# ScalarE's exponentials in the step of their scores, and index scores, compressed scores and compressed values in fewer or halved matmuls, in a three-block transformer kernel

## What is computed

```python
# layer 0, "AB": sparse latent attention (8 heads) beside a forgetting attention (8 heads)
rel = relu(einsum('bqhd,bsd->bqhs', qi, k_idx))        # index scores: 8 heads of 64
score = einsum('bqhs,bqh->bqs', rel, wi)
_, idx = top_k(score, n_keep)                          # 64 keys per query
o_lat = softmax(q_abs . ckv[idx] + q_rot . k_rope[idx]) . ckv[idx]
o_b = softmax(q . k * scale + cum_q - cum_k) . v       # causal

# layer 1, "C": three branches for 16 heads in 2 groups, mixed by gates
s_c = einsum('bqghd,bngd->bghqn', qb, kc) * scale      # kc, vc: 15 compressed keys/values
p_c = masked_softmax(s_c, cmp_end <= t)
o_c = einsum('bghqn,bngd->bqghd', p_c, vc)
o_s, o_w = selected and window attention, both causal over 256 keys here
out = g0 * o_c + g1 * o_s + g2 * o_w

h = h + square(relu(u @ w1)) @ w2                      # MLP after layers 0 and 1
# then a differential attention layer with 16 heads, w_in 1024 x 8192, w_out 2048 x 1024
```

## Time and profile before

| | |
|---|---|
| time, median of 3 runs | 922.86 us (922.78 to 924.11) |
| the profiled execution: its own time | 921.05 us |
| its span | 919.2 us |
| granted TensorE clock, mean | 1.00 of full speed |
| PE busy | 902.2 us, 98% |
| DVE busy | 648.4 us, 71% |
| ACT busy | 513.6 us, 56% |
| POOL busy | 133.0 us, 14% |
| HBM | 158 GB/s over the span |

### The profile page before, as it was taken

One profiled execution on the slowest core, in us unless ns is written; L12 is line 12 of the kernel. 1 busy time (PEld: TensorE's weight loads), 2 busy tenths in 40 slices (PEclk: granted clock), 3 DMA queues, 4 the chain that ended last, 5 costly groups with the idle time before them and its releaser, 6 DMA issues. The chain is left out here.

```text
span 919.2 us, 14875 instructions
## 1 busy us (share of the span) xinstructions
PE 902.2 (98%) x4853; PEld 753.0 (82%) x4853; DVE 648.4 (71%) x1175; ACT 513.6 (56%) x1019; POOL 133.0 (14%) x190
## 2 busy tenths in 40 slices
PE   8999999999999999999999999999999999999998
PEld 7878788888888878898888888888887788878876
DVE  4769656666666679866567666666887878777785
ACT  6654546544544466566454454454556666666573
POOL 3310200000000010245310000000430400400401
PEclk9999999999999999999999999999999999999999
DMA  9644024655555556400246555555464344454431
GB/s 365 224 141 163 19 93 139 207 197 190 186 192 193 183 170 208 151 1 1 94 148 211 190 188 191 193 183 189 154 206 155 127 154 162 155 176 150 160 115 47
DMA packets 40521, 146.39 MB, mean 159 GB/s; under 512 B 4496, under 2 KB 4752, under 8 KB 40464
## 3 DMA queue, kind: packets, MB, share of 16 engines
q1 hardware_dynamic: 40176, 145.43, 47.6%
q10 hardware_dynamic: 288, 0.21, 0.1%
HBM read 144.57 MB, written 1.05 MB: 158 GB/s over the span
## 5 line engine op out<-in xcount | busy, mean ns | idle before, releaser
L450 DVE TENSOR_TENSOR wl<-raw,wh 128x1024 fp32r<-128x1024 f32 x269 | 330.3, 1232 | 138.2 <-ACT wh L445 132.5
L445 ACT ACTIVATE wh<-raw 128x1024 fp32r<-128x1024 f32 x270 | 284.5, 1057 | 152.8 <-PE acc L347 132.3
L345 PE MATMUL acc<-wh,xhl 128*128 128x512 f32 (+1 forms) x472 | 191.9, 407 | 1.4 <-DVE wl L450 1.4
L347 PE MATMUL acc<-wh,xhl 128*128 128x512 f32 (+1 forms) x472 | 184.3, 391 | 0.0
L346 PE MATMUL acc<-wl,xhl 128*128 128x512 f32 (+1 forms) x472 | 183.8, 389 | 0.0
L345 PEld LDWEIGHTS acc<-wh,xhl 128*128 128x128 f32 x472 | 88.7, 188 | 24.8 <-issue 6.2
L347 PEld LDWEIGHTS acc<-wh,xhl 128*128 128x128 f32 x472 | 88.6, 188 | 19.3
L346 PEld LDWEIGHTS acc<-wl,xhl 128*128 128x128 f32 x472 | 88.8, 188 | 17.3 <-issue 1.0
L345 PE MATMUL acc<-wh,hh 128*128 128x512 f32 x256 | 100.8, 394 | 0.0
L346 PE MATMUL acc<-wl,hh 128*128 128x512 f32 x256 | 100.4, 392 | 0.0
L347 PE MATMUL acc<-wh,hl 128*128 128x512 f32 x256 | 100.1, 391 | 0.0
(11 more groups left out here) (318 smaller groups left out, 1333.3 us busy)
## 6 DMA issues: line engine op xcount, KB each, us to landing
raw<-stream SPq DMA_DIRECT2D x270, 512.0 KB, 3.3
h<-x SPq DMA_DIRECT2D x2, 512.0 KB, 4.7
out<-h SPq DMA_DIRECT2D x4, 256.0 KB, 2.1
row<-rows SPq DMA_DIRECT2D x1, 700.0 KB, 11.8
probs<-sel SPq DMA_DIRECT2D x1, 512.0 KB, 10.6
cst<-consts SPq DMA_DIRECT2D x1, 507.0 KB, 9.8
col<-cols ACTq DMA_DIRECT2D x1, 138.5 KB, 5.5
cst<-consts ACTq DMA_DIRECT2D x1, 64.0 KB, 4.3
```

The source lines that it names most:

```text
L345: nc.tensor.matmul(out_, ah, bh, start=start, stop=False, skip_group_check=True)
L347: return nc.tensor.matmul(out_, al, bh, start=False, stop=stop_, skip_group_check=True)
L445: nc.scalar.activation(wh[:, u % SPLIT, :], raw[:, u % RAW, :], ACT.Copy).then_inc(w_hi, 1)
L450: nc.vector.tensor_tensor(wl[:, u % SPLIT, :], raw[:, u % RAW, :], wh[:, u % SPLIT, :].bitcast(F32), ALU.subtract).then_inc(w_lo, 1)
```

## The change

- Both loops: ACT takes the exponentials of step `it` in its own step `it`, behind the copy `p_first(it - 2)`, where it took those of `it - 1`. ACT's copy of a projection result (`evac`) in step 1 is ahead of the exponentials of step 1.
- Index scores: each head has a matmul of its own on its 64 rows, 128 and 256 columns, into a bank of its own. The index key is stored twice in one tile and turned once (two transposes for four). ACT's `relu` reads 384 columns of either bank.
- Compressed scores: the 16 heads are in two banks of eight, `acc[2]` and `acc[3]`, each with its mask matmul; the high and low parts of the keys are 32 columns of one matmul, and the two parts stand beside each other in the bank. DVE adds them with two reductions each in steps 5 and 8. Heads 0 to 3 are ahead of the second transposes of step 2, heads 4 to 7 in step 3; heads 8 to 11 are ahead of the second transposes of step 7 and wait for all query parts, heads 12 to 15 are at the end of step 7. The softmax reads SBUF and has 16 columns per head, of which one is padding.
- Compressed values: 128 rows for 120; each matmul of 512 columns is two of 64 rows and 256 columns, for different banks. Both query tiles run in step 11 for one half of the heads and in step 13 for the other, none in step 14.

```diff
+NC = N_CMP + 1
+PAD = -2.0 ** 99
...
-            (ptp, [[kid[:, t, a, :] for t in range(T)] for a in range(2)]),
+            (ptp, [[kid[:, t].rearrange("p a d -> p (a d)") for t in range(T)]]),
...
         def idx_scores(y):
...
-            for t, bank in ((0, pair[y % 2]), (1, (misc, ptp)[y % 2])):
-                n = (t + 1) * P
-                last = mm(bank[:, 0:2 * n].rearrange("p (a k) -> p a k", a=2),
-                          QK[:, B_QI + y, t * P:(t + 1) * P], QK[:, B_KI:B_KI + 2, 0:n],
-                          start=True, stop=True, skip_group_check=True)
-            last.then_inc(idx_scored, 1)
+            for t, k0, nk in TK:
+                for a, bank in enumerate((pair[y % 2], (misc, ptp)[y % 2])):
+                    rows = slice(a * HD, (a + 1) * HD)
+                    last = mm(bank[:, k0:k0 + nk], QK[rows, B_QI + y, t * P:(t + 1) * P], QK[rows, B_KI, 0:nk],
+                              start=True, stop=True, skip_group_check=True)
+                    if t == T - 1:
+                        last.then_inc(idx_scored, 1)
...
         def scores(st, q, keys, bias):
...
+        def compressed_scores(heads):
+            if heads[0] % HPG == 0:
+                mm(cmp_bank(heads[0] // HPG)[:, :, :, 0, :], idr[:, :],
+                   unseen[:, :, :].unsqueeze(2).broadcast_to([P, T, HPG, NC]), start=True, stop=False,
+                   skip_group_check=True)
+            for n in heads:
+                for t in range(T):
+                    last = mm(cmp_bank(n // HPG)[:, t, n % HPG, :, :], c_q(n)[:, 0, t * P:(t + 1) * P],
+                              kcs[:, n % CG, :, :], start=False, stop=True, skip_group_check=True)
+            if heads[-1] % HPG == HPG - 1:
+                last.then_inc(cmp_scored, 1)
         def c_iter(it):
...
+            if it == 2:
+                pe.wait_ge(dve_prep, 10)
+                pe.wait_ge(ev_act, left(G_CO))
+                pe.wait_ge(ev_dve, left(G_CO))
+                compressed_scores(range(0, 4))
+            if it == 7:
+                pe.wait_ge(q_lo, 12)
+                compressed_scores(range(8, 12))
...
+            if it == 3:
+                compressed_scores(range(4, 8))
+            if it == 7:
+                compressed_scores(range(12, 16))
             if it in (3, 5):
...
-            if it in (2, 3, 5, 7):
-                z = (2, 3, 5, 7).index(it)
-                if z == 0:
-                    pe.wait_ge(dve_prep, 10)
-                    pe.wait_ge(ev_act, left(G_CO))
-                    pe.wait_ge(ev_dve, left(G_CO))
-                    for t in range(T):
-                        mm(acc[2][:, t * SEQ:(t + 1) * SEQ].rearrange("p (h n) -> p h n", n=NC), idr[:, :],
-                           unseen[:, t, :].unsqueeze(1).broadcast_to([P, STEPS_C, NC]), start=t == 0, stop=False,
-                           skip_group_check=True)
-                if z >= 2:
-                    pe.wait_ge(q_lo, 6 + 2 * z)
-                for n in range(4 * z, 4 * z + 4):
-                    for t in range(T):
-                        c0 = (t * STEPS_C + n) * NC
-                        for part in range(2):
-                            last = mm(acc[2][:, c0:c0 + NC], c_q(n)[:, 0, t * P:(t + 1) * P],
-                                      kcs[:, n % CG, part, :], start=False, stop=part == 1,
-                                      skip_group_check=True)
-                if z == 3:
-                    last.then_inc(pe_prep, 1)
             if it == 10:
...
-                    last = nc.tensor.transpose(acc[3][0:HPG * N_CMP, k * P:(k + 1) * P],
-                                               pc[:, k * HPG * N_CMP:(k + 1) * HPG * N_CMP], ident)
+                    last = nc.tensor.transpose(acc[3][:, k * P:(k + 1) * P], pc[:, k * P:(k + 1) * P], ident)
...
-            for at_it, t, half in ((11, 0, 1), (11, 1, 1), (13, 0, 0), (14, 1, 0)):
-                if it == at_it:
-                    if half == 1:
-                        pe.wait_ge(dve_prep, 12)
-                    else:
-                        pe.wait_ge(o_seeded, t + 1)
+            if it in (11, 13):
+                half = (13 - it) // 2
+                if half == 1:
+                    pe.wait_ge(dve_prep, 12)
+                else:
+                    pe.wait_ge(o_seeded, 2)
+                for t in range(T):
...
-                    mm(acc[2 + t][:, :], pct[:, k * P:(k + 1) * P], vcb[:, :],
-                       start=True, stop=True, skip_group_check=True).then_inc(pe_prep, 1)
+                    for r in range(2):
+                        rows, cs = slice(64 * r, 64 * r + 64), slice(SEQ * r, SEQ * r + SEQ)
+                        mm(acc[2 + r][:, t * SEQ:(t + 1) * SEQ], pct[rows, k * P:(k + 1) * P], vcb[rows, cs],
+                           start=True, stop=True, skip_group_check=True).then_inc(pe_prep, 1)
...
         def first_steps(uu):
...
         def relu(y):
...
-            act.wait_ge(idx_scored, y + 1)
...
-            s_.activation(probs[:, y % 2, 0:2 * P], pair[y % 2][:, 0:2 * P], ACT.Relu)
-            s_.activation(probs[:, y % 2, 2 * P:2 * P + 2 * SEQ], (misc, ptp)[y % 2][:, :],
-                          ACT.Relu).then_inc(idx_relu, 1)
+            for a, bank in enumerate((pair[y % 2], (misc, ptp)[y % 2])):
+                act.wait_ge(idx_scored, 2 * y + a + 1)
+                last = s_.activation(probs[:, y % 2, a * KEYS:(a + 1) * KEYS], bank[:, 0:KEYS], ACT.Relu)
+            last.then_inc(idx_relu, 1)
...
         def turned_out(z, dst, scale=1.0):
...
-            s_.activation(dst.rearrange("p c s -> p (c s)"), AB_Z[z][0][:, :], ACT.Copy,
+            s_.activation(dst.rearrange("p c s -> p (c s)"), AB_Z[z][0][:, 0:dst.shape[1] * SEQ], ACT.Copy,
...
         def keys_out(z, dst):
...
-        for it in range(1, STEPS_AB + 2):
+        for it in range(STEPS_AB + 2):
...
-            if it - 1 < STEPS_AB:
-                exponentials(it - 1)
+            if it == 1:
+                evac(act, G_VB, U_ABO, 0, Y[:, 0, BV:BV + GW], rr(N_A0), GW)
+            if it < STEPS_AB:
+                exponentials(it)
...
-            if it == 1:
-                evac(act, G_VB, U_ABO, 0, Y[:, 0, BV:BV + GW], rr(N_A0), GW)
...
-        for it in range(1, STEPS_C + 2):
+        for it in range(STEPS_C + 2):
...
-            if it - 1 < STEPS_C:
-                exponentials(STEPS_AB + it - 1)
+            if it == 1:
+                evac(act, G_C + 3, U_CQ2 + 4, 0, Y[:, 0, CQ + GW:CQ + 2 * GW], rr(N_A1), GW)
+            if it < STEPS_C:
+                exponentials(STEPS_AB + it)
...
-            if it == 1:
-                evac(act, G_C + 3, U_CQ2 + 4, 0, Y[:, 0, CQ + GW:CQ + 2 * GW], rr(N_A1), GW)
             if it in (4, 6):
...
             if it == 9:
...
             if it == 12:
-                for t in range(T):
-                    act.wait_ge(pe_prep, 7 + t)
-                    s_.activation(o_tok[:, t, 512:1024], acc[2 + t][:, :], ACT.Copy).then_inc(o_seeded, 1)
+                act.wait_ge(pe_prep, 9)
+                for r in range(2):
+                    s_.activation(o_tok[:, :, 512 + SEQ * r:512 + SEQ * (r + 1)],
+                                  acc[2 + r][:, :].rearrange("p (t d) -> p t d", t=T), ACT.Copy).then_inc(o_seeded, 1)
...
             if it in (4, 6):
...
+            if it in (5, 8):
+                b = it // 8
+                dve.wait_ge(cmp_scored, b + 1)
+                parts = acc[2 + b][:, :].rearrange("p (t h a n) -> p t h n a", t=T, h=HPG, a=2)
+                for t in range(T):
+                    v_.tensor_reduce(pc5[:, t, b], parts[:, t], AX.X, ALU.add).then_inc(parts_added, 1)
             if it == 8:
-                dve.wait_ge(pe_prep, 5)
-                seen_scores = acc[2][:, :].rearrange("p (h n) -> p h n", n=NC)[:, :, 0:N_CMP]
-                ch.link(v_.tensor_reduce(cmx, seen_scores, AX.X, ALU.max))
+                dve.wait_ge(parts_added, 2 * T)
+                ch.link(v_.tensor_reduce(cmx, pcall, AX.X, ALU.max))
...
-                v_.tensor_tensor(pcall, seen_scores, over_keys, ALU.subtract).then_inc(dve_mid, 1)
+                v_.tensor_tensor(pcall, pcall, over_keys, ALU.subtract).then_inc(dve_mid, 1)
             if it == 9:
...
             if it == 10:
-                dve.wait_ge(pe_prep, 6)
-                v_.tensor_copy(pct[:, :], acc[3][0:HPG * N_CMP, :]).then_inc(dve_prep, 1)
+                dve.wait_ge(pe_prep, 5)
+                v_.tensor_copy(pct[:, :], acc[3][:, :]).then_inc(dve_prep, 1)
             if it in (13, 14):
-                t = it - 13
-                dve.wait_ge(pe_prep, 9 + t)
+                r = it - 13
+                dve.wait_ge(pe_prep, 13)
...
-                v_.tensor_tensor(o_tok[:, t, 0:512], acc[2 + t][:, :], o_tok[:, t, 0:512],
+                os = o_tok[:, :, SEQ * r:SEQ * (r + 1)]
+                v_.tensor_tensor(os, acc[2 + r][:, :].rearrange("p (t d) -> p t d", t=T), os,
```

(7 more changed lines are left out.)

42 lines of the change are left out of this document (22 added, 20 removed).

## The result

The changed kernel takes **930.0 us** as the median of 20 runs (923.9 to 933.4); the kernel before takes 922.6 as the median of 20 (920.9 to 924.5). The ratio is 1.0069, with a 95% interval of 1.0055 to 1.0083: slower by 0.7%, 7.4 us. I had forecast 924.8 with a range up to 926.8. The direction was right, the size was not.

A forecast was written before the change was run, and what follows sets the result against it. TensorE's instruction stream plus its idle moments was taken to bound the kernel. Terms -0.9 - 0.2 + 0.4 + 2.6 = +1.9 us gave 923.0 for a profiled execution, 924.8 as a median, range 921.0 to 926.8.

The forecast's parts named there:

- Compressed scores, 3.6 us: PE, four score groups: 32-column matmuls cost 0.111 us like 16-column ones, each group loses 0.89 us, 3.6 saved.
- Compressed values, 1.2 us: PE, layer 1's value groups: 64-row halves side by side take 1.2 us for 1.77 or 1.83, 1.2 saved.
- Index scores and key transposes, 0.9 and 0.2: PE: four index steps take 1.06 us each for 1.29, 0.9 saved; two transposes for four save 0.2.
- Rival 2: Index scores and values: halves cost nothing at their ends, factor of two in full; 922.4 us, no change; chance 0.08.
- rival 3: Layer 1: value halves don't run side by side, DVE's strided reductions take 0.6; whole +3.5, 926.4 us; chance 0.13.
- Layer 0's loop, +0.4: Layer 0, steps 2 and 3: ACT's copy behind the exponentials reaches PE late, +0.4 us; DVE's 1.47 wait stays.
- Steps 2 and 3, 5 and 7: Layer 1's loop: new PE waits and moved score groups give +0.5 us (steps 2 and 3), -0.9 (5), +1.5 (7).
- Steps 8 and 9: Layer 1's loop: DVE's two reductions add +0.8 us in step 8, DVE's wait for ACT's exponential +1.0 in step 9.
- Step 12 on: Layer 1's loop: PE waits 0.8 us behind ACT's output copies; +1.1 with step 13's longer values, -0.8 in step 14.
- The loop's sum, +2.6: Layer 1's whole loop: 7.4 us of new waits against 4.8 of shorter work, +2.6 us; bounds +1.8 or +4.2.
- Rival 1: Both loops: ACT's order does not hold PE, only the shorter stream counts; whole -3.0, 919.8 us; chance 0.16.
- Rival 4: Built program: the change doesn't do what it says, ACT's order is as before; chance 0.03.

The follow-up runs named there:

- e8: Kernel before plus five matmuls of zeros in step 10 and two in step 11 of layer 1's loop: 922.58 us, ratio 1.0001.
- e9: Kernel before with only the index scores changed (two key transposes for four included): 921.43 us, ratio 0.9985.
- e5: Changed kernel plus matmuls of zeros ahead of seven PE waits in layer 1's loop: 925.17 us, ratio 1.0029.
- e10: Kernel before with ACT's new order in layer 0's loop alone: 923.34 us, ratio 1.0003.
- e2: Changed kernel with ACT's old order of exponentials put back in both loops: 922.02 us, ratio 0.9989.
- e11: Changed kernel plus matmuls of zeros in step 3 of layer 1's loop alone, 6 and 8: 927.83 us, ratio 1.0048.
- e3: Kernel before with nothing changed but ACT's new order in both loops: 935.32 us, ratio 1.0147.
- e7: Changed kernel with ACT's old order, compressed scores late in steps 2 and 7, plus matmuls of zeros in steps 10 and 11: 917.74 us, ratio 0.9944.

## Why the prediction was wrong

**The step that failed** is the one from the profiled execution to the median: "The sum is made against the profiled execution, 921.05 us, which is 1.8 us below the median [...]; I add the difference to the median". I took these 1.8 us for a constant that the change leaves alone. They are for the most part a loss of clock: the profiled execution of before ran at 1.00 throughout, its usual run at 0.998, with a fall near 407 in the profiles of e8 and e9 (921.6 at full clock, 922.8 over all 31 runs). In the changed kernel the same difference is 930.0 - 924.0 = 6.0 us, because new idle time stands in a loop where the clock falls now and then already. The prediction has no term for this: it priced every wait at its own length and every duration at 2.4 GHz. The one profile of before gave no sign of it, since the clock stayed at 1.00 behind the wait of 1.47 us in layer 0 and the one of 2.25 us in the last block; one execution could not rule it out. Of the miss of 5.2 us, 4.2 arise in this step (6.0 for 1.8) and 1.0 in the sum for full clock (923.0 forecast, 924.0 measured). Against the filled kernel e5, the clock costs 4.8.

**Of the bookkeeping**, at full clock (forecast +1.9, profiled span +2.7):

- *Compressed scores, 3.6 us.* Right. The four groups take 0.83 (384.28 to 385.11), 0.90, 0.80 and 0.89; forecast 0.89 each. A matmul of 32 columns holds PE for 0.10 to 0.11 us, like one of 16. The Trainium skill, "TensorEngine Tiling (Array Packing)", section "Instruction Overhead", would have put it at an estimated 25 ns; the trace does not agree.
- *Compressed values, 1.2 us.* A group takes 1.06 (424.47 to 425.53), forecast 1.2: 1.4 to 1.5 saved in all.
- *Index scores and key transposes, 0.9 and 0.2.* Right: 1.05 for a step, and e9 measures 1.4 us for both (0.4 to 2.4 by its interval). The factor of two of the Trainium skill, "TensorEngine Tiling (Array Packing)", section "Theoretical Speedup", would have given 2.8; the trace does not agree, with 1.29 us for a step before and 1.05 now. Rival 2 is out by this, and rival 3 by the value group of 1.06 and the reductions of 0.39 us each.
- *Layer 0's loop, +0.4.* Right in size: in the changed kernel's trace the loop, from its first scores to its last transposes, takes 33.93 us (86.23 to 120.16) for 33.45 (87.54 to 120.99), +0.48; e10's runs are too few to tell. The waits lie elsewhere than I had them: the 1.47 for DVE, which I let stand, is gone, and 0.79 for ACT's copy, 0.74 for DVE's and 0.54 for ACT's stand in its place.
- *Steps 2 and 3, 5 and 7.* Waits of 0.74, 1.07, 0.90 and 1.19 us, forecast 0.95, 1.15, 1.0 and 1.4; each ended by the engine and line named. With the 0.43 of step 2 that I did not have, the loop is 1.3 us behind at the first transposes of step 8 (408.51 against 407.94, counted from the loop's start), and I had +1.1.
- *Steps 8 and 9.* The two reductions take 0.78 to the next start (forecast 0.74), DVE waits 0.97 for ACT's exponential (forecast 1.0). These are the rows of DVE:

```profile
412.04 0.75 DVE L2361 TENSOR_REDUCE va<-acc 128x128 f32<-128x256 f32 x2
412.82 0.69 DVE L2364 TENSOR_REDUCE sml<-va 128x32 f32<-128x512 f32 x1
...
417.39 0.69 DVE L2369 TENSOR_REDUCE sml<-va 128x32 f32<-128x512 f32 x1 [0.97 <-ACT va L1651]
```

- *Step 12 on.* A wait of 0.66, forecast 0.8.
- *The loop's sum, +2.6.* It is +3.5. At the transposes of step 10 the changed kernel is 2.3 us behind, counted from the loop's start (416.23 - 377.55 against 414.67 - 378.26), and I had +1.9; at those of step 11 it is 3.7 behind (421.46 against 418.48), and I had +2.9. So of the 0.9 us that are missing 0.2 arise ahead of step 8 and the rest in steps 8 to 10, on the chain through DVE: the wait there is 1.62, and two of 0.20 and 0.29 us follow at 417.88 and 419.98 that my queues did not have.

**Rival 1**, that ACT's order does not hold PE, is refuted by e2: with the old order 5.1 us go at full clock, 8.0 in the median. Rival 4 is out by the same run.

**What stays open.** Why an execution falls into one, two or all three slow stretches and another into none is not settled; the program is the same, and so is the wait of 0.43 us ahead of the first fall, 6.54 us behind the loop's start with a fall and without (383.99 - 377.45 and 384.09 - 377.55). How much of the loss each of the three stretches brings is not separated either, beyond the 2.2 us of e11. Why the half clock lasts 3.4 us behind one wait and 20 behind another in e3 is not shown; the most that the rows say is that PE's work behind that wait is narrow. Nor did I run the changed order with only `exponentials` or only the projection copy moved.

## What to carry to other kernels

Taking work off the bounding engine pays only as long as its partners deliver in time: here 5 us of matmuls were saved, and an order on ScalarE that puts a ready but unneeded piece (this step's exponentials) ahead of the one TensorE waits for (the copy of the turned probabilities) gave back as much at full clock (5.1 us) and 8.0 in the median. Ask of every piece that is moved forward on an in-order engine who waits for what it now stands in front of. And where a loop of short matmuls gets new waits of about 1 us, don't price them at their own length: look at the granted clock over several executions, not one, and where the profiled one is faster than the median ask first whether that gap is clock and whether the change will widen it.

## What the runs showed of the hardware

- TensorE's granted clock fell to half behind waits of only 0.4 to 1.7 us, in a loop of short matmuls, for 3.3 to 20 us at a time. In layer 0's loop it did so behind 0.79 and 0.74 us in two profiles (e10, e11), while in the profile of before it stayed full behind 1.47 us. In the last block it stayed full behind 2.2 us and more in 12 of 14 profiles. Without a wait it fell behind groups of 16-column matmuls (e8, e9, e10) and of 32-column ones (e7).
- Matmuls of zeros into an idle bank, 54 of them in seven places, kept it at 0.996 to 1.00 and made the kernel 4.8 us faster while adding 6.8 us to PE's busy time (903.9 for 897.1). Taking the cause of the waits away was worth more than filling them (917.4 against 925.2), and on top of that the fill brought nothing (917.7).
- Over the runs of one kernel time goes with the mean clock: those of the changed kernel from 924.0 at 1.00 to 930.0 at 0.992 and 933.4 at 0.987, some 0.7 us for each thousandth.
